# Output products of a chunked SSM on TensorE: groups taken two at a time, row halves alternating

## The reference, cut to what matters

```python
_, _, x_re, x_im = lax.associative_scan(_ssm_combine, (a_re, a_im, bu_re, bu_im), axis=1)
y = (jnp.einsum('blgp,ghp->blgh', x_re, c_re.astype(f32))
     - jnp.einsum('blgp,ghp->blgh', x_im, c_im.astype(f32))
     + uf * d.astype(f32).reshape(SSM_GROUPS, SSM_GROUP))
g = jax.nn.gelu(y.reshape(Bsz, L, SSM_WIDTH))
out = g * jax.nn.sigmoid(g @ glu_w.astype(f32) + glu_b.astype(f32))
```

## Time and profile before

| | |
|---|---|
| device time, median of 3 | 1241.51 us (1241.5 to 1242.51) |
| the profiled execution: its own time | 1242.07 us |
| its span, first to last instruction | 1240.2 us |
| mean granted TensorE clock | 0.964 |
| PE matmul busy | 1141.3 us, 92%, 5022 records |
| PE weight loads busy | 548.9 us, 44% |
| DVE / ACT / POOL busy | 468.8 / 360.1 / 289.6 us |
| DMA | 261.95 MB, mean 211 GB/s |

### The profile page before, as it was taken

One profiled execution on the slowest core, in us unless ns is written; L12 is line 12 of the kernel. 1 busy time (PEld: TensorE's weight loads), 2 busy tenths in 40 slices (PEclk: granted clock), 3 DMA queues, 4 the chain that ended last, 5 costly groups with the idle time before them and its releaser, 6 DMA issues.

```text
span 1240.2 us, 16198 instructions
## 1 busy us (share of the span) xinstructions
PE 1141.3 (92%) x5022; PEld 548.9 (44%) x5023; DVE 468.8 (38%) x1003; ACT 360.1 (29%) x731; POOL 289.6 (23%) x227
## 2 busy tenths in 40 slices
PE   6999999998899999983799999988999999999990
PEld 5897444464356666653333333322333333333330
DVE  3550039932455666317333233222322323323313
ACT  3121100015455555400122332322223223232223
POOL 0110299910000000100221222222122122122123
PEclk9999999999899999995899999989999999999996
DMA  7127111012411111186492799999889999999317
GB/s 252 27 40 136 34 35 35 0 68 73 170 47 56 52 52 52 52 322 238 160 408 72 289 375 375 418 408 411 328 323 382 389 408 377 402 380 393 116 21 274
DMA packets 86157, 261.95 MB, mean 211 GB/s; under 512 B 31927, under 2 KB 49086, under 8 KB 61518
## 3 DMA queue, kind: packets, MB, share of 16 engines
q1 hardware_dynamic: 68868, 243.43, 51.0%
q0 software_dynamic: 11520, 16.81, 6.1%
q10 hardware_dynamic: 5706, 0.92, 0.4%
HBM read 244.86 MB, written 26.74 MB: 219 GB/s over the span
## 4 chain that ended last, share of the span: by engine, by line
PE 87%; DMA 4%; DVE 3%; ACT 2%; issue 1%; DVEq 1%; POOL 0%; SPq 0%; ACTq 0%; POOLq 0%
PE psum L1304 27%; PE psum L1323 13%; PE psum L1029 13%; PE psum L1215 9%; PE psum L1026 4%; PE psum L1173 3%; DMA W<-in_w_gate 3%; PE psum L1292 3%; PE psum L1193 2%; PE psum L1024 2%; PE psum L1311 2%; PE psum L1184 2%; PE psum L1237 1%; DMA W<-in_x 1%; PE psum L1229 1%
## 5 line engine op out<-in xcount | busy, mean ns | idle before, releaser
L1304 PE MATMUL psum<-W,RD 128*64 x800 | 369.2, 605 | 14.2 <-DVE RD L1791 14.2
L1305 PE MATMUL psum<-W,RD 128*64 128x512 f32 x800 | 369.2, 605 | 0.0
L1304 PEld LDWEIGHTS psum<-W,RD 128*64 128x64 f32 x800 | 106.7, 139 | 226.0 <-issue 220.1
L1323 PE MATMUL psum<-W,RD 128*64 x400 | 184.0, 603 | 2.2 <-ACT RD L952 2.2
L1324 PE MATMUL psum<-RD 128*64 128x512 f32 x400 | 184.1, 603 | 0.0
L697 POOL DMA_INDIRECT x_rows<-RD,tabi x49 | 79.4, 1621 | 447.7 <-ACT RD L959 438.0
L1772 DVE TENSOR_TENSOR RD<-psum,RD 128x256 f32<-128x256 f32 x50 | 21.2, 425 | 415.5 <-ACT RD L948 415.5
L1029 PE MATMUL psum<-W 128*128 128x512 f32 x384 | 166.4, 593 | 0.6 <-ACT W L782 0.6
L1215 PE MATMUL psum<-W,RD 128*128 128x512 f32 x256 | 119.3, 600 | 5.3 <-DVE W L1589 4.2
L1029 PEld LDWEIGHTS psum<-W 128*128 128x128 f32 x384 | 72.5, 190 | 89.7 <-issue 88.7
L1305 PEld LDWEIGHTS psum<-W,RD 128*64 128x64 f32 x800 | 106.7, 139 | 0.0
(11 more groups left out here) (319 smaller groups left out, 1263.9 us busy)
## 6 DMA issues: line engine op xcount, KB each, us to landing
W<-in_w_up SPq DMA_DIRECT2D x32, 2048.0 KB, 13.2
W<-in_w_gate SPq DMA_DIRECT2D x32, 2048.0 KB, 18.3
W<-in_w_down SPq DMA_DIRECT2D x32, 2048.0 KB, 20.3
W<-in_x SPq DMA_DIRECT2D x16, 512.0 KB, 4.7
W<-in_w_in SPq DMA_DIRECT2D x5, 1024.0 KB, 11.6
W<-in_w_in SPq DMA_DIRECT2D x16, 256.0 KB, 4.3
x_rows<-W SPq DMA_DIRECT2D x8, 512.0 KB, 2.9
h_rows<-RD SPq DMA_DIRECT2D x8, 512.0 KB, 3.5
```

The costliest lines, as they stand in the source:

```text
L1304: pe.matmul(bank(2)[0:HALF].rearrange("p (g n) -> p g n", g=2), x, near, start=k == 0, stop=k == KD - 1)
L1305: ins = pe.matmul(bank(2)[HALF:P], x, upgate1[:, k].rearrange("p g n -> p (g n)"), start=k == 0, stop=k == KD - 1)
L1323: pe.matmul(out[0:HALF], a, W[:, bass.ds(base + (2 * KD * FF + D * k), 512)], start=k == 0, stop=k == FK - 1)
```

## The change

The loop over 16 groups with three products each becomes a loop over 8 pairs with six products each: real part of the even group (partitions 0 to 63), real part of the odd group (64 to 127), both imaginary parts in the same order, and then the two products of 128 rows. The products, their operands, the PSUM addresses and the two increments of `y_ps` (after pair 3 and after pair 7, as after groups 7 and 15) are the same.

```diff
             pe.wait_ge(scan_ok, 1)
             pe.wait_ge(toep_in, 16 * CHUNK)
-            for g in range(GROUPS):
-                a, q = g // 2, STATES * (g % 2)
-
-                b, c = 2 * (g % 2) + g // 8, (g // 2) % 4
-                out = psum[:, b, P * c:P * c + P]
-                pe.matmul(out, XR[q:q + STATES, a, :], CAR[q:q + STATES, a, 1:CHUNK + 1, :].rearrange("p t h -> p (t h)"),
-                          start=True, stop=False)
-                pe.matmul(out, XI[q:q + STATES, a, :], CAI[q:q + STATES, a, 1:CHUNK + 1, :].rearrange("p t h -> p (t h)"),
-                          start=False, stop=False)
-                ins = pe.matmul(out, UT[:, g, :], TG[:, g, :], start=False, stop=True)
-                if g % 8 == 7:
+            for a in range(PAIRS):
+                out = [psum[:, 2 * r + a // 4, P * (a % 4):P * (a % 4) + P] for r in range(2)]
+                for X, CA, first in ((XR, CAR, True), (XI, CAI, False)):
+                    for r in range(2):
+                        q = slice(STATES * r, STATES * r + STATES)
+                        pe.matmul(out[r], X[q, a, :], CA[q, a, 1:CHUNK + 1, :].rearrange("p t h -> p (t h)"),
+                                  start=first, stop=False)
+                for r in range(2):
+                    ins = pe.matmul(out[r], UT[:, 2 * a + r, :], TG[:, 2 * a + r, :], start=False, stop=True)
+                if a % 4 == 3:
                     ins.then_inc(y_ps, 1)
```

## The result

| | before | after |
|---|---|---|
| median, six executions each | 1242.55 us (1241.5 to 1243.44) | 1235.43 us (1233.12 to 1238.55) |
| the profiled execution: time / span | 1242.07 / 1240.2 us | 1235.06 / 1233.2 us |
| stage, first output product to the unit behind it | 16.81 us | 10.20 us |
| PE matmul busy | 1141.3 us | 1134.6 us |

The account below looks back on a forecast made before the run. It took TensorE, matmul-busy for 92% of the span, to bound the kernel. Savings of 3.2 us and 3.4 us, together 6.7, took 1242.07 to 1235.4; the median stands 0.56 lower, so 1234.8 us, range 1232.0 to 1238.5.

Parts of the forecast that it names:

- The bound: Whole kernel: TensorE never waits in the changed stage, so shortening that stage shortens the kernel; 6.7 us less.
- The two terms: Output-product stage: 16 fewer changes of shape at 0.20 save 3.2 us; overlap of the row halves saves 3.4 us.
- The first rival, strict order: Within a pair: records start and end in program order, one slot more, 0.9 us given back, 1235.7 us; chance 0.09.
- No overlap: Within a pair: loads or reads bind, 12 slots and two changes, only 3.2 us saved, 1238.3 us; chance 0.08.
- a price for each change of half: Three changes of half within a pair each cost like a change of shape; stage 1.5 us longer, 1243.0; chance 0.03.
- What hangs on the stage's end: Behind the stage: add, table and gelu end some 4.6 us later, under the unit's 6.88 us, leaving 2.3 us cover.
- The clock downstream: Behind the stage: one low-clock stretch more, 1238.9 us, chance 0.04; one fewer, 1230.7 us, chance 0.03.

Follow-up runs that it names:

- same half (2): Against the changed kernel, the four 64-row products between two changes of shape all lie on one half, still 16 changes: 1241.72 us, ratio 0.9986.
- four changes (3): Against the changed kernel, one 128-row product put between a pair's real and imaginary parts, so 32 changes of shape: 1238.69 us, ratio 0.9964.
- the change (1): The changed kernel run again with no edit: 1235.49 us, ratio 0.9941.
- blocked (4): Against the changed kernel, both parts of a pair's even group first, then both of the odd group: 1238.63 us; run again, 1235.85 us.
- two pairs (5): Against the changed kernel, two pairs at a time, 8 changes of shape: 1236.38 us; then with DVE's layer norm ahead of both adds: 1233.92 us.

## Why the prediction was right, point by point

**The bound.** The stage lay on the chain with nothing of another engine in it, and what it lost the kernel gained: forecast 1234.8 us, measured 1235.43, inside the range of 1232.0 to 1238.5. The stage lost 6.61 us of the 6.7 forecast.

**The two terms.** The forecast split 6.7 us into 3.2 for sixteen fewer changes of shape and 3.4 for overlap. Experiments 2 and 3 each keep one of the two, and kernels with the same 96 records give both prices by themselves. With a slot (128 columns, one or both halves) of 0.110 us and a change of shape of 0.197 us, both fitted to these stages:

| kernel | slots / changes | computed | measured stage |
|---|---|---|---|
| before | 96 / 32 | 16.9 | 16.81 |
| same half (2) | 96 / 16 | 13.7 | 13.71 |
| four changes (3) | 64 / 32 | 13.3 | 13.34 |
| the change (1) | 64 / 16 | 10.2 | 10.20 |
| blocked (4) | 64 / 16 | 10.2 | 10.25 |
| two pairs (5) | 64 / 8 | 8.6 | 8.63, 8.62 |

Thirty-two slots fewer are 3.5 us and sixteen changes fewer 3.15 us, together 6.7, measured 6.61. The slot had been taken as 0.1075 from wide products and the change as 0.20; in the saving those errors nearly cancel. They do not in every order: the forecast's prices would give 13.5 us for the same half, where 13.71 was measured.

**The first rival, strict order.** It was priced at 0.9 us, and the pair would have taken 1.37 us; it took 1.29. The blocked order settles it more plainly, since there strict order would cost 2.7 us, and the stage is only 0.05 us longer. Two 64-row halves work off their records side by side over at least four records of each. Whether the records of one half keep their order was not tested. The rule of the Trainium skill, *TensorE: Matmul & The Clock Gate*, Part 3, that matmuls start and end strictly in program order, is not borne out by these runs, as I had applied it to the two halves.

A change of shape costs 0.197 us, and a change of half nothing that the stages show: with one change of half a pair (blocked) the stage is no shorter than with three. That agrees with the Trainium skill, *TensorEngine Tiling (Array Packing)*, "Key Properties", by which changing the tiling mode drains TensorE and changing only the tile does not.

**No overlap, and a price for each change of half.** Both fell, as the earlier trace rows had said: the pattern of the scores carried over to eight records in a row and to sums that are added to. The loads overlap as the matmuls do (eight of 0.18 to 0.19 us within 0.52).

**What hangs on the stage's end.** The times of DVE came as worked out, each 0.5 us later (270.3 and 275.4 forecast, 270.81 and 275.89 read): 0.26 us is the later entry, and the rest is mostly the step from PE's last product to DVE's start, which the forecast left out. So the chain to the gelu's end is 4.77 us and not 4.6, as it already was in the earlier trace rows, and the cover of 2.3 us was 2.1. The two-pairs kernel shows where it ends: with adds, norm and gelu in a row it is 1.7 us short.

**The clock downstream.** It had been a rival of 4.1 us up or down in one case out of fourteen. The mechanism is there and of that size: 4.4 to 4.6 us between two executions of one kernel. But it had been tied to the change, and the stretch near 320 us comes or goes from one execution of the same kernel to the next. It is one part of the scatter (1230.56 to 1238.55 for the changed kernel over all runs); the rest is not accounted for. How many of the executions without a trace had it is not known, so it is in part luck that the medians were not moved by it. In the profiled pair the longer stretch took 1.2 us of the gain in the attention, and the routing gave as much back. What fixes whether an execution has it stays open; no run here was made for it.

**The median of before.** It was 1241.51 us from three executions, and 1242.55 from six. The gain of 7.1 us is 0.5 us above what the stage gave. Single executions scatter by more than that, so nothing is to be explained in it. In part, then, it is luck that 1234.8 and 1235.43 lie so close: from the later median the same 6.7 us would have given 1235.9.

## What to carry to other kernels

Products of 64 rows that alternate with products of 128 cost twice: for every change of shape, and for the idle half of the array. Count slots and changes separately: priced from the one trace of before, they gave the changed stage to 0.1 us (10.1 for 10.20) and the others to 0.2. Before stretching such a batch over more output banks, count who gets its input later: here another 1.6 us off the stage on TensorE was worth nothing until VectorE's order was changed with it.

## What the runs showed of the hardware that was not expected

The halves need no strict alternation: with four records of one half and then four of the other, eight records took 0.65 us, as with alternation by products. And the 0.197 us of a change of shape can be read as two parts: about 0.10 us of a record's own weight load (374 or 377 ns for the first record of a piece where the median is 272 or 275), and 0.09 to 0.10 us between the last record of a piece and the next shape. The second part shows at the end of the stage, where the unit has the same shape as the products ahead of it: the last four records of 128 rows take 0.55 us (275.14 to 275.69) instead of 0.64, and the last two of experiment 3 take 0.32 (278.61 to 278.93) instead of 0.42. That it is the emptying of the array is a reading; the split was not tested by itself.
